# Inside block 2's attention steps, TensorE's dealt products go ahead of the values' product and VectorE's dealt work goes ahead of the scaling

## The reference

```
hq, hf, hi, hg, sq, sk, sv, iq, ik, iw, mq = split_in(h @ w_in[layer])
o_hg  = hgrn2_mix(hq, hf, hi, hg, lb, out_gain)         # ends with rmsnorm * silu(g)
score = sum_h iw[h] * relu(iq[h] . ik)                  # top 128 keys of each query are kept
o_sa  = softmax(norm(sq) . norm(sk) / 8, kept keys) @ sv    # 4 heads of 64
o_mem = softmax(norm(mq) . norm(km) / 8) @ vm               # 4 heads of 64, 256 keys
x = x + concat(o_hg, o_sa, o_mem) @ w_out
```

## Time and profile before

| | |
|---|---|
| time, median of 3 runs | 1625.55 us (1625.21 to 1625.95) |
| the profiled execution: its time | 1623.29 us |
| the profiled execution: its span | 1621.5 us |
| mean granted TensorE clock in it | 0.989 |
| the loop of block 2's attentions in it, from the first S to the last scale | 1095.52 us to 1207.4 us |
| busy in the span: TensorE, VectorE, ScalarE | 97%, 56%, 39% |

### The profile page before, as it was taken

The page is one execution under the profiler, slowest core; times in us unless marked ns, Lnnn a source line. Parts: engine busy times, 40 slices in busy tenths (PEclk is TensorE's granted clock), DMA queues, the critical chain, the costliest instruction groups (busy, mean ns, idle before and its releaser), DMA issues.

```text
span 1621.5 us, 20637 instructions
## 1 busy us (share of the span) xinstructions
PE 1565.8 (97%) x7842; PEld 1309.7 (81%) x7842; DVE 900.9 (56%) x1442; ACT 625.0 (39%) x861; POOL 11.8 (1%) x16
## 2 busy tenths in 40 slices
PE   7999999999998999999999889998899999999999
PEld 7887877888876788888888758998888788888887
DVE  5444476445454777777423767988865434444322
ACT  6441334332233444444323544565563322323211
POOL 0000000000000000000000000000000000000000
PEclk9999999999998999999999999999999999999999
DMA  9312220322222122222422312111002222222222
GB/s 346 124 53 104 76 75 27 110 98 103 104 78 104 39 93 102 103 103 78 155 101 81 119 52 85 72 36 71 27 27 104 80 102 103 94 87 103 104 104 78
DMA packets 25885, 150.24 MB, mean 93 GB/s; under 512 B 2611, under 2 KB 5043, under 8 KB 9436
## 3 DMA queue, kind: packets, MB, share of 16 engines
q1 hardware_dynamic: 25820, 149.35, 25.7%
HBM read 147.21 MB, written 2.13 MB: 92 GB/s over the span
## 4 chain that ended last, share of the span: by engine, by line
PE 84%; DVE 8%; ACT 4%; issue 2%; DMA 1%; SPq 0%; DVEq 0%; ACTq 0%
PE bank L1709 26%; PE bank L1711 25%; PE bank L1710 25%; ACT w_hi L584 2%; PE bank L1823 2%; PE bank L2113 1%; PE bank L1803 1%; PE bank L2050 1%; DVE w_lo L1057 1%; DVE sel L1485 1%; DVE st L1484 1%; DMA x<-xT 1%; PE bank L1812 1%; DMA raw<-weights 1%; DVE w_lo L1065 1%
## 5 line engine op out<-in xcount | busy, mean ns | idle before, releaser
L1709 PE MATMUL bank<-h_hi,w_hi 128*128 128x512 f32 (+1 forms) x1200 | 475.9, 397 | 10.5 <-DVE h_lo L1130 9.2
L1057 DVE TENSOR_TENSOR w_lo<-raw,w_hi 128x2048 fp32r<-128x2048 f32 x118 | 270.3, 2291 | 364.1 <-ACT w_hi L584 363.7
L1711 PE MATMUL bank<-h_hi,w_lo 128*128 128x512 f32 (+1 forms) x1200 | 469.4, 391 | 0.0
L1710 PE MATMUL bank<-h_lo,w_hi 128*128 128x512 f32 (+1 forms) x1200 | 469.1, 391 | 0.0
L584 ACT ACTIVATE w_hi<-raw 128x2048 fp32r<-128x2048 f32 x128 | 244.4, 1910 | 346.4 <-PE bank L1711 344.3
L1709 PEld LDWEIGHTS bank<-h_hi,w_hi 128*128 128x128 f32 (+1 forms) x1200 | 225.7, 188 | 64.8 <-DVE h_lo L1130 9.0
L1711 PEld LDWEIGHTS bank<-h_hi,w_lo 128*128 128x128 f32 (+1 forms) x1200 | 225.6, 188 | 48.9
L1710 PEld LDWEIGHTS bank<-h_lo,w_hi 128*128 128x128 f32 (+1 forms) x1200 | 226.0, 188 | 47.1 <-issue 0.9
L1709 PE MATMUL bank<-a_hi,w_hi 128*128 128x512 f32 x352 | 136.9, 389 | 0.0
L1710 PE MATMUL bank<-a_lo,w_hi 128*128 128x512 f32 x352 | 136.9, 389 | 0.0
L1711 PE MATMUL bank<-a_hi,w_lo 128*128 128x512 f32 x352 | 136.9, 389 | 0.0
(11 more groups left out here) (282 smaller groups left out, 1905.3 us busy)
## 6 DMA issues: line engine op xcount, KB each, us to landing
raw<-weights SPq DMA_DIRECT2D x128, 1024.0 KB, 4.8
toep<-bias_scratch SPq DMA_DIRECT2D x8, 448.0 KB, 4.5
x<-xT SPq DMA_DIRECT2D x2, 1024.0 KB, 9.7
x_tok<-x_tok SPq DMA_DIRECT2D x1, 2048.0 KB, 11.7
outT<-x SPq DMA_DIRECT2D x8, 256.0 KB, 4.4
mem_tok<-mem_tok SPq DMA_DIRECT2D x1, 1024.0 KB, 10.8
mem2T<-mem2T SPq DMA_DIRECT2D x1, 1024.0 KB, 5.7
memT<-memT SPq DMA_DIRECT2D x2, 256.0 KB, 3.7
```

Source lines behind the costliest of these rows:

```text
L1057: nc.vector.tensor_tensor(w_lo[m % 2][:, :], raw[m % 2][:, :], w_hi[m % 2][:, :].bitcast(F32), ALU.subtract).then_inc(lo_ready, 1)
L1709: nc.tensor.matmul(o, lh, rh, start=first, stop=False)
L1710: nc.tensor.matmul(o, lh, rl, start=False, stop=False)
L1711: return nc.tensor.matmul(o, ll, rh, start=False, stop=last)
```

## The change

In the steps of `mem_2`, and only there, `between(s)` is called earlier: on TensorE between T(s-3) and O(s-4), on VectorE between L1198 and scale(s-4). ScalarE's stream stays as it is. No instruction is added or taken away, and the first block's attentions keep their order. Line numbers behind the edits move by 2 on VectorE, by up to 4 on TensorE.

```
@@ VectorE, attention() @@
                         nc.vector.tensor_scalar(mx[:, w % 8, 1:2], mx[:, w % 8, 0:1], scale, None, ALU.mult
                                                 ).then_inc(neg_max, 1)
+                    if kind == "mem_2":
+                        between(s)
                     if s >= LAG + 1:
...
                         frees(("O", w), nc.vector.tensor_scalar(d, B(("O", w))[:, 0:d.shape[-1]], mx[:, w % 8, 3:4],
                                                                 None, ALU.mult))
-                    if between is not None:
+                    if between is not None and kind != "mem_2":
                         between(s)
```

## The result

The changed kernel takes 1630.59 us (median of 8 runs, 1628.06 to 1632.9); the kernel before took 1624.78 as the median of 8 runs (1623.71 to 1625.95), the three of the table above among them. The ratio is 1.0035, with a 95% interval of 1.0024 to 1.0046: slower, by 5.8 us where 3.7 were forecast. The runs lie over 4.8 us and those of before over 2.2; but 33 runs of before, made for later comparisons, lie over 5.8, so the width says little.

What follows compares the result with a forecast made beforehand. VectorE was taken to set the pace up to step 24, TensorE then carrying the end. Costs of 0.8 + 0.4 + 0.4 + 0.6 + 1.5 = 3.7 us on 1625.55 gave 1629.3 us; 8-in-10 range 1627.0 to 1631.3.

Steps and rivals of the forecast that it cites:

- What bounds the stage: Loop of block 2's attentions: VectorE's work sets the pace up to step 24; TensorE's waits before O echo it.
- Items 1 and 2: Steps 8 and 16: scale now behind `w_lo`, 0.8 us on VectorE; step 24: O(21) behind the second `o_hg`, 0.4 us.
- Items 3 to 5: Step 28, scale(24) behind the root's wait, 0.4 us; steps 29 to 31, O(25) waits, 0.6; drain stretches, 1.5.
- the walk: The step-by-step sum of the five costs through the loop, 3.7 us in all, with nothing for low clock.
- VectorE's four `w_hi` idles stay as they are: Sign that the forecast is right: VectorE's four waits for ScalarE's `w_hi`, 5.9 us in all, do not change.
- rival C: Longer waits before O bring the 1.2 GHz clock; after O(25) 0.9 to 1.5 us more, 1630.2 to 1630.8; chance 0.15.
- item 1: Steps 8 and 16: scale(4) and scale(12) leave the wait for `w_hi` and cost VectorE 0.39 us each, 0.8 us.
- the mechanism's low end of 1628.4: Lower edge of the forecast's own range, 1628.4 to 1630.9 us for the whole kernel.
- The 1.0 us and 0.6 us that were held back: Possible extra, taken as 0: O directly behind P, 1.0 us; RECIPROCAL behind the search at steps 8, 16 and 24, 0.6 us.

Runs made afterwards that it cites:

- third experiment: The change, but at steps 8, 16 and 24 VectorE scales ahead of its dealt work as in the kernel before: 1630.94 us, ratio 1.0039 against the kernel before.
- the fifth: The kernel before up to step 27, with the change's order on both engines from step 28 on: 1627.24 us, ratio 1.0023 against the kernel before.
- the filled kernel: The changed kernel with 12 useless matmuls ahead of the second `o_hg` and 12 ahead of O(25): 1627.5 us, ratio 1.0018 against the kernel before.

## Why the prediction was right, and where it fell short

- **What bounds the stage: right.** TensorE is the busiest engine of the stretch, but filling its waits for scales won nothing in two kernels, and ending three idle times of VectorE won 0.15%. The first is the weaker evidence, since the filled waits came back as other waits; the second is what shows that VectorE sets the pace up to step 24. The Trainium skill, Perfetto Trace Analysis, section Identifying the Most-Contended Engine, would have the engine with the highest occupancy optimised first. Read as work on TensorE's own order, these runs disagree for this stage: ratio 1.0007 against 0.9985.
- **Items 1 and 2, right in size.** S(9) 28.4 us after S(0) instead of 28.0, S(17) 51.9 instead of 51.1, S(25) 81.7 instead of 80.6: 0.4, 0.8 and 1.1 late. The second `o_hg` was forecast at 1175.75 from S(0) at 1095.52; with S(0) 1.22 later that is 1176.97, and it was 1176.89. Putting the three scales back (third experiment) restored the old distances of VectorE.
- **Items 3 to 5, right in size.** 2.5 forecast, 2.6 in the loop when only steps 28 and later were changed. O(25) is the first O to wait. O(31) was forecast at 1209.65; with the 1.22 and 3.1 for the low clock that is 1213.97, and it started at 1213.96. (The 3.1 was taken from the loop's length, so this row checks the end of the walk and not the 3.1; the filled waits are what checks that.)
- **"VectorE's four `w_hi` idles stay as they are": not quite.** They grew, from 1.05 to 1.44 us at step 8 and from 5.9 to 7.1 in sum, by the 0.39 of the scale that no longer lies in that time. The cost per step was right; it stands in the profile as idle time, since `w_hi` did not come sooner.
- **The clock: the term that was mis-sized.** The sum had 0 for it, and rival C allowed it a single time, behind O(25), with a chance of 0.15 and a price of 0.9 to 1.5 us. It came three times in the profiled execution. The three waits that rival C named, before O(5), O(13) and O(25), were 2.06, 1.79 and 1.78 us long. The first low stretch, from 1126.7, was covered, as rival C had said: S(16) is taken no later than item 1 makes it. The other two cost time, behind O(25) and behind the second `o_hg`, whose wait had been 1.56 us long without consequence in the trace of before. The price of each was 1.5 to 1.7, the upper end or a little more.
- **The evidence on the clock was read too narrowly.** The prediction counted two waits of about 1.5 us and one low clock, and took that as evidence against. The trace of before has four waits of TensorE of 1.4 us and more in the loop (before a T at 1105.51, O(6), an O at 1147.58, `o_hg`), and one was followed. Over all eleven profiles, before and after and the nine experiments, it is 18 of 44, and 18 of 33 without the first one of each loop, which never was; the shortest wait with a low clock behind it was 1.47 us, the longest without 2.76. So each of the two uncovered waits should have had its own chance of about a half. On the average that adds 1.5 us to the forecast, 1630.8, and with both stretches 3 us, 1632.3; 1630.59 was measured.
- **Where luck helped.** The forecast was 3.7 us above a median of before of 1625.55, from three runs; from eight it is 1624.78. So the time came out 1.3 us too low and the difference 2.1. The range of 1627.0 to 1631.3 held the result, though its edges, and the mechanism's low end of 1628.4, are not worked out from any row.

What stays open: why the low clock follows one wait and not another of the same length; and how much of the median, and not of one profiled execution, each stretch makes. The low clock falls at different places in each execution (ahead of the loop in one, three times in it in another), with one profile for each kernel. The 1.0 us and 0.6 us that were held back for O behind P and for RECIPROCAL did not show: the loops of the third, the fifth and the filled kernel lie within 0.2 us of the walk.

## What to carry to other kernels

When two engines hand work to each other, find what an engine waits for behind an instruction before you move it later. If it filled that wait and the wait's end doesn't move, it now costs its full time (0.39 us a scale here). Where the two engines only pass work to and fro, as at the end of this loop, what is put ahead of a handover makes the relay longer (here by 1.6 us, with four scalings of 1.05 us put ahead of four scales). Filling the busiest engine's waits was worth nothing where another engine set the pace: they came back as other waits; follow the wait back to the first engine that rests for something else (here `w_hi` on ScalarE) and start that earlier. And give each new uncovered wait of TensorE of this size a chance of a stretch at low clock, about a half here, at its full price, one by one.

## What the runs showed of the hardware

- Behind waits of TensorE of 1.83 and 1.78 us the granted clock was 0.50 (1.2 GHz) for about 3.4 us, at the cost of 1.5 to 1.7 us each: 118.4 against 115.1 us of loop with the two waits filled. In another execution it stayed at 1.00 behind waits of 1.77, 1.82, 2.25 and 2.76 us. Of the 44 waits of 1.4 us or more in the loops of all profiles, 18 were followed by it.
- TensorE work that computes nothing made a kernel faster: 24 matmuls of 256 columns more, and the median went from 1630.59 to 1627.5 us.
- VectorE's order alone cost 23.4 us and both orders together 5.8, so that the smaller edit is the dearer one.
